# Gate products and transposes moved in a two-block fp32 transformer kernel

## What is computed

```python
for l in range(DEPTH):                       # DEPTH = 2
    h = rms_norm(x, norm_g[l]) * (1 + sc[:, None]) + sh[:, None]
    hc = rms_norm(ctx, norm_g[l]) * (1 + sc_c) + sh_c
    qa, ka, va, ga, qb, kb, vb, gb, qn, kn, vn, gn = split_proj(h @ w_in[l])
    ...
    # differential heads: 4 heads, each of two softmaxes
    s = jnp.einsum('bqhmd,bkhmd->bhmqk', q, k) * (q.shape[-1] ** -0.5)
    p = jax.nn.softmax(s, axis=-1)
    a = p[:, :, 0] - lam * p[:, :, 1]
    oa = jnp.einsum('bhqk,bkhd->bqhd', a, v)
    ya = (rms_norm(oa, diff_subln[l]) * (1 - lam_init)) * jax.nn.silu(ga)
    ...
    # grouped heads: 6 query heads on 2 key and value heads
    qb = axial_rope(rms_norm(qb, gqa_q_norm[l]), row, col)
    kb = axial_rope(rms_norm(kb, gqa_k_norm[l]), row, col)
    yb = gqa_attend(qb, kb_all, vb_all) * jax.nn.silu(gb)
```

## Time and profile before

| | us |
|---|---|
| median of 3 runs (3630.17 to 3630.45) | 3630.39 |
| the profiled execution | 3630.19 |
| its span from first to last instruction | 3628.4 |
| PE busy in the span | 3522.4 (97%) |
| DVE busy | 2281.5 (63%) |
| ACT busy | 1269.9 (35%) |
| POOL busy | 1041.2 (29%) |

### The profile page before, as it was taken

How to read it: one execution, slowest core, us unless ns; L and a number is a source line. 1 busy time by engine, 2 the same in 40 slices (tenths; PEclk the granted TensorE clock), 3 DMA queues, 4 the chain that set the end, 5 groups by cost and what they waited for, 6 DMA issues and landing times. The chain is left out here.

```text
span 3628.4 us, 53906 instructions
## 1 busy us (share of the span) xinstructions
PE 3522.4 (97%) x20756; PEld 2533.3 (70%) x20756; DVE 2281.5 (63%) x4223; ACT 1269.9 (35%) x2394; POOL 1041.2 (29%) x981
## 2 busy tenths in 40 slices
PE   7999998999999999989999999999999999999999
PEld 4656546789754655567898568655755588888888
DVE  4377454765675377557656662575648777894488
ACT  3255434532632255446425321575332211001100
POOL 2400063666541500256665430001324200000000
PEclk9999999999999999999999999999999999999999
DMA  5101143001112101110011221000000377552254
GB/s 200 50 18 42 48 156 102 2 1 42 54 62 93 47 18 42 65 36 1 2 41 55 82 82 36 24 24 24 24 24 30 111 275 259 186 190 89 93 186 162
DMA packets 142267, 279.01 MB, mean 77 GB/s; under 512 B 5728, under 2 KB 50784, under 8 KB 139584
## 3 DMA queue, kind: packets, MB, share of 16 engines
q1 hardware_dynamic: 114848, 221.89, 17.6%
q10 hardware_dynamic: 25872, 47.71, 3.7%
q0 software_dynamic: 1296, 5.97, 0.4%
HBM read 231.52 MB, written 44.04 MB: 76 GB/s over the span
## 5 line engine op out<-in xcount | busy, mean ns | idle before, releaser
L1003 PE MATMUL ps<-ring,hT 128*128 128x512 f32 (+3 forms) x1296 | 375.8, 446 | 9.6 <-DVE nrm_b L1184 4.4
L1003 PEld LDWEIGHTS ps<-ring,hT 128*128 128x128 f32 x1296 | 217.9, 191 | 145.9 <-issue 122.9
L1544 DVE TENSOR_REDUCE stat_a<-ps 128x1 f32<-128x1280 f32 (+1 forms) x144 | 190.7, 1366 | 154.0 <-PE ps L1388 154.0
L1442 PE MATMUL ps<-hT,ring 128*128 128x512 f32 (+1 forms) x640 | 280.2, 551 | 0.0
L1753 POOL TENSOR_TENSOR P_b<-P_b,stat_b 128x1280 f32<-128x1280 f32 (+1 forms) x108 | 227.9, 2132 | 173.5 <-DVE stat_b L1769 136.8
L2842 ACT ACTIVATE hid<-hid 128x1024 f32<-128x1024 f32 x32 | 33.9, 1058 | 482.3 <-DVE hid L2889 410.5
L1484 ACT ACTIVATE YT<-ps,stat_a 128x1280 f32<-128x1280 f32 (+1 forms) x144 | 176.6, 1232 | 25.4 <-DVE stat_a L1544 25.4
L2669 PE MATMUL ps<-Y 128*128 128x256 f32 x768 | 171.1, 379 | 0.9 <-DVE Y L2654 0.5
L1528 POOL COPY rb_a<-stat_a 128x64 f32<-128x64 f32 x72 | 14.7, 238 | 538.9 <-DVE YT L1557 538.9
L2669 PEld LDWEIGHTS ps<-Y 128*128 128x128 f32 x768 | 145.8, 190 | 21.3 <-issue 1.5
L1413 PEld LDWEIGHTS ps<-const,YT 128*128 128x128 f32 x656 | 71.6, 142 | 97.4 <-issue 86.5
(11 more groups left out here) (616 smaller groups left out, 8127.0 us busy)
## 6 DMA issues: line engine op xcount, KB each, us to landing
ring<-in_w_up SPq DMA_DIRECT2D x16, 2048.0 KB, 9.0
ring<-down_sums SPq DMA_DIRECT2D x16, 2048.0 KB, 8.1
ring<-in_w_in SPq DMA_DIRECT2D x14, 2048.0 KB, 8.1
ring<-in_w_down SPq DMA_DIRECT2D x12, 2048.0 KB, 8.4
adaw_b<-in_w_ada SPq DMA_DIRECT2D x16, 1024.0 KB, 5.2
ring<-in_w_out SPq DMA_DIRECT2D x6, 2048.0 KB, 7.9
Wd<-in_w_down ACTq DMA_DIRECT2D x11, 1024.0 KB, 7.4
down_sums<-Wd ACTq DMA_DIRECT2D x11, 1024.0 KB, 7.6
```

The source lines that it names most:

```text
L1003: mm = pe.matmul(ps[:, bank(n), 0:hi - lo], hT[:, k, t * P:(t + 1) * P], w[:, k, lo:hi], start=(k == 0), stop=(k == KC - 1))
L1442: mm = pe.matmul(ps[:, GB, 0:hi - lo], pr.view(i0 + c)[:, k, b % 4 * P:(b % 4 + 1) * P], hT[:, k, lo:hi], start=(k == 0), stop=(k == KC - 1))
L1544: dve.tensor_reduce(st[:, i % 4, m:m + 1], scored_at(i, m), AX, ALU.max, negate=True)\
```

## The change

Two tables change. In `stage_diff`, in both layers, one product is taken from each of steps 1 to 8 of the table into the one before, and then once more from each of 2 to 10 into the one before. The first two entries end up with five products, entries 8 and 10 with three, all others keep four, and from entry 11 on everything stands as before. In the grouped projection of layer 1 the transposes of the ten units stand two units earlier (unit 5's one unit earlier): behind units 2, 3, 4, 5, 6, 8, 10, 13, 14, 15, where they were behind 4, 5, 6, 7, 8, 9, 12, 15, 16, 17.

```diff
@@ -1320,6 +1320,9 @@
             quanta += [[(i, k) for k in range(4)], [(i, k) for k in range(4, KC)]]
         else:
             quanta.append([(i, k) for k in range(KC)])
+    for more, less in ((0, 8), (1, 10)):
+        for s in range(more, less):
+            quanta[s].append(quanta[s + 1].pop(0))
     assert len(quanta) == n
@@ -4062,7 +4065,7 @@
-        banks=lambda sb: (0, 1, 6, 7) if last else (0, 1), later=lambda sb: (2, 4, 4, 4) if last else (), ...
+        banks=lambda sb: (0, 1, 6, 7) if last else (0, 1), later=lambda sb: (-2, -2, -2, -2, -2, -1, 0, 2, 2, 2) if last else (), ...
```

More of the change, by code:

```diff
@@ L4064, in layer @@
         "copy": {"chunk": 1, "lo": 0, "hi": 128, "dst": V}}, BANK, True,
-        banks=lambda sb: (0, 1, 6, 7) if last else (0, 1), later=lambda sb: (2, 4, 4, 4) if last else (), raw=lambda sb: (YT[:, 2:KC, 0:width], io["spill"][:, 2:KC, 0:width]), sub=norm_of_a,
+        banks=lambda sb: (0, 1, 6, 7) if last else (0, 1), later=lambda sb: (-2, -2, -2, -2, -2, -1, 0, 2, 2, 2) if last else (), raw=lambda sb: (YT[:, 2:KC, 0:width], io["spill"][:, 2:KC, 0:width]), sub=norm_of_a,
         silu=lambda sb: [YT[:, k, 0:pieces[-1][1]] for k in range(2, 5)], **({} if last else {"ada": modulate}))
```

## The result

The changed kernel takes **3674.65 us** (median of 4 runs, 3671.72 to 3675.21) against 3630.28 beside it (4 runs, 3628.23 to 3630.45): 1.0121 times as long, 95% interval [1.0109, 1.0133]. The prediction was 3674.3, range 3655 to 3686. The profiled execution took 3674.45 us, its span is 3672.6, the mean granted clock 0.993 (before 0.996).

What follows compares the result with a forecast made beforehand. PE was taken to bound stage_diff. From 3630.2 us, +34.8 for both layers' stalls and moved products, +13.5 for clock falls and -4.2 for the grouped projection gave 3674.3 us, range 3655 to 3686.

Steps and rivals of the forecast that it cites:

- Step 0: stage_diff: the fourth of five products waits for ACT's copy of piece 0, made after both exps; +2.3 us.
- Steps 2, 4 and 6: stage_diff: the third product waits for ACT's copy, which stands behind both exps; 3.2 us each, 9.6 a layer.
- Step 8: stage_diff: PE waits for ACT's copy before the last product; +2.1 us.
- Steps 7 and 9: stage_diff: all three products follow the last transposes instead of filling the waits between them; +1.7 us each, 3.4 a layer.
- Steps 1 and 3: stage_diff: these steps keep four products and their waits; nothing added.
- The clock: Both stage_diff stages: nine of 14 new stalls followed by a fall to half the granted clock, 1.5 us each; +13.5 us.
- rival that every stall costs a fall: Clock falls after every stall, or a stage after a fall makes DVE and ACT late; 3680 to 3690 us, chance 0.12.
- rival of the held clock: PE's clock holds at the new gaps, nought to four falls; 3660.8 us, up to 3667, chance 0.20.
- filled gaps: Rival: four gaps take a product each of 0.86 us and the projection gives all 6.8; 3620.0 us, chance 0.03.
- The grouped projection: Layer 1: earlier transposes let POOL run ahead, shortening PE's waits; -4.2 us, the middle of 3.1 and 5.2.

Runs made afterwards that it cites:

- e3: Changed kernel with ACT's copy of a gate piece that ends inside a step put ahead of that step's two exps: 3647.04 us, 1.0044 times before.
- e6: Changed kernel with only the first loop of the table edit, so one product per step moves, not two: 3650.34 us, 1.005 times before.
- e4: Changed kernel with the three products of steps 7 and 9 cut 1, 2, 0 around the transposes instead of 0, 0, 3: 3664.59 us, 1.0091 times before.
- e2: Kernel before with only the gates' products moved, in both layers, transposes as before: 3676.44 us, 1.0128 times before.
- e7: e4 with unneeded matmuls put into PE's idle time ahead of the waiting product in steps 0, 2, 4 and 6: 3655.82 us, 1.0069 times before.
- e8: Kernel before with only the transposes of layer 1's grouped projection moved, one unit earlier instead of two: 3628.51 us, 0.9993 times before.
- e9: The e8 kernel unchanged, run again for a second profile: 3628.28 us, 0.9991 times before.
- e1: Kernel before with only the transposes of layer 1's grouped projection moved as in the change: 3628.68 us, 0.9993 times before.

## Why the prediction was right

**Step 0** (+2.3): 2.32 and 2.31. **Steps 2, 4 and 6** (+3.2 each): 3.19 in step 4 of layer 0, which is free of a fall; the others have the same 2.93 us of idle time. The step from "ACT's copy stands behind both exps" to "PE waits for it" is shown by e3, which moves only that. **Step 8** (+2.1): 2.08 in both layers. **Steps 7 and 9** (+1.7 each): 9.71 less a fall of 1.7 is 1.71 over 6.30, and e6, whose step 7 has no fall in layer 0, has 8.02 - 6.30 = 1.72. **Steps 1 and 3** (nothing): 0.02 and 0.00. In sum 34.8 us, as forecast. The mechanism was right, step by step. It could be worked out to a tenth because every duration and the order of both engines stand in the trace before; only the order was new.

**The clock** (+13.5, 9 of 14 stalls, 1.5 each): eight of 14, and 47.5 - 34.8 = 12.7 us, 1.6 for each. The sum is nearly right by two small errors that go against each other, and the reason was half right. The prediction took longer gaps to be more likely followed by a fall. The falls came behind four of the six stalls of 2.93 us and all four of steps 7 and 9, whose idle time is 0.78 and 1.74, and behind none of step 0's 2.19 and step 8's 1.86. In e4, with the same stalls of steps 0, 2, 4 and 6, one of step 0's was followed by a fall. Length alone doesn't decide it. The number nine was a choice between "none" and "all", and a kernel shifted by a few us can give another total: e2 took 1.8 us more than the changed kernel, though its projection alone should make that 5.2. The rival that every stall costs a fall is out with 8 of 14. That idle gaps are the cause e7 bears out. In the example of the Trainium skill's page "TensorE: Matmul & The Clock Gate" (section "HAM oscillation — how this bites in real kernels") PE's waits between bursts of matmuls are the cause too, and there every burst behind one starts at the half rate; here 8 of 14 did. The rival of the held clock (3660.8) is out, and so are the filled gaps (3620.0): the earlier trace rows's 0.93 us did fill, four times, and it bought nothing because the stall behind was larger.

**The grouped projection** (-4.2, between 3.1 and 5.2): the stage gained 5.15, so the term was mis-sized by 1 us, and PE's idle time there fell from 6.76 us (2.38 + 1.52 + 2.86) to 1.82. The upper value came out, but its reason, that the small operations get shorter when POOL is ahead, holds only in part. What the sum left out is that DVE had waited for POOL already at units 4 and 5 of the kernel before:

```profile
1554.91 0.69 DVE L1184 TENSOR_TENSOR nrm_b<-ps,st_b 128x512 f32<-128x512 f32 x1 [1.38 <-POOL rot_b L1285]
...
1563.08 0.69 DVE L1184 TENSOR_TENSOR nrm_b<-ps,st_b 128x512 f32<-128x512 f32 x1 [0.49 <-POOL rot_b L1285]
...
1578.43 0.69 DVE L1184 TENSOR_TENSOR nrm_b<-ps,st_b 128x512 f32<-128x512 f32 x1
```

The scalings of units 7, 8 and 9 in the changed kernel:

```profile
1624.43 0.69 DVE L1184 TENSOR_TENSOR nrm_b<-ps,st_b 128x512 f32<-128x512 f32 x1
...
1629.17 0.29 DVE L1184 TENSOR_TENSOR nrm_b<-ps,st_b 128x128 f32<-128x128 f32 x1
...
1631.67 0.29 DVE L1184 TENSOR_TENSOR nrm_b<-ps,st_b 128x128 f32<-128x128 f32 x1
```

Unit 7 is scaled 65.11 us after the stage's start (1624.43 - 1559.32), where it was 66.80 (1578.43 - 1511.63): 1.7 us earlier, which the sum, starting at unit 8, doesn't have. From there unit 8 took 4.74 us, longer than the 3.8 of the forecast (its small operations are no shorter than before, up to 0.94 us), and unit 9 took 2.50, shorter than 3.8 by its small operations, 0.16 to 0.53. Together 1.7 - 0.9 + 1.3 = 2.1 us over the 3.1. In e8 the small operations of unit 9 are up to 0.86 long, and the stage is shorter still. That the term would in the end hardly reach the kernel's end, when it is alone, the prediction didn't see at all.

**The total** (3674.3 against 3674.65) is closer than its terms: the clock's term was 0.8 us too large, the projection gave 1.0 more than forecast, and 1.8 us came in stages that the prediction put at nothing. That these three cancel to a few tenths is luck; that the time lies near the middle of the range is not.

## What to carry to other kernels

In an engine that works in order, an idle gap can be filled only by work whose own release comes earlier than the gap. Before moving work forward, look at what it waits for, and at what stands ahead of that in the *other* engine's order: here moving products into gaps of 0.93 us put in a wait for a copy that stands behind two exps, and cost up to 3.2 us in each of several later steps. A division such as `len(part) // 4` changes a step's whole shape when its count goes from four to three; look for such places when a table is edited.

A gain of some us in one stage of a kernel like this is measured at the stage, and can be lost behind it to the clock; judge it by both.

## What the runs showed of the hardware

- A wait of 1.9 to 2.9 us on PE, or two of 0.78 and 1.74 close together, can cost 1.6 us more than itself, by a stretch at half the granted clock behind it. It did so in 8 of 14 cases, and not by length. Filling eight such waits with matmuls that nobody needs took 8.8 us off the kernel; in the profiles the two stages are 7.3 us shorter.
- Most falls come back at the same places in two executions of one program (2676, 2748 and 2775 us in e8 and e9; 2680 and 2744 to 2745 in both profiles of the kernel before; but one was at 591 us in the first of these and at 580 in the second), and move when the program is shortened by 4 us ahead of them. The same idle gap of 2.80 us, released by the same operation, was followed by seven us near half the clock in one and by three in the other. That took 3.9 of 5.7 us of a gain made 1000 us earlier.
- The best kernel measured is e8's, transposes one unit earlier and nothing else: 3628.51 and 3628.28 us against 3630.41 and 3630.45. The second's 0.9991, [0.9982, 1.0], is at the edge of what can be told from no change, and e1's 3628.68 can't be told from it.
